# VectorE makes all low parts of the weights in two passes

## The reference, cut to what matters

```python
def conv_ffn(x, w_in, conv_w, conv_b, w_out):
    h = causal_depthwise_conv(x @ w_in, conv_w, conv_b)
    val, gate = jnp.split(h, 2, axis=-1)
    return (jax.nn.silu(gate) * val) @ w_out
...
        h = rms_norm(x, norm_mix_g[layer])
        if m == 0:
            y = pool_mixer(h, pool_w[j], pool_b[j], pool_scale[j])
        x = x + y.astype(x.dtype)
        f = conv_ffn(rms_norm(x, norm_ffn_g[layer]), ffn_w_in[layer], ffn_conv_w[layer], ffn_conv_b[layer], ffn_w_out[layer])
        x = x + f.astype(x.dtype)
```

## Time and profile before

| | |
|---|---|
| median of three runs | 2387.79 us |
| profiled execution | 2391.25 us, span 2389.5 us |
| TensorE busy | 2289.1 us, 96% |
| VectorE busy | 1600.5 us, 67% |
| ScalarE busy | 1313.9 us, 55% |
| GpSimd busy | 752.2 us, 31% |
| low parts on GpSimd (L2820) | 496.1 us in the page's largest group, 638 instructions |

### The profile page before, as it was taken

One profiled execution on the slowest core, in us unless ns is written; L12 is line 12 of the kernel. 1 busy time (PEld: TensorE's weight loads), 2 busy tenths in 40 slices (PEclk: granted clock), 3 DMA queues, 4 the chain that ended last, 5 costly groups with the idle time before them and its releaser, 6 DMA issues.

```text
span 2389.5 us, 35445 instructions
## 1 busy us (share of the span) xinstructions
PE 2289.1 (96%) x11782; PEld 1941.9 (81%) x11782; DVE 1600.5 (67%) x3239; ACT 1313.9 (55%) x3030; POOL 752.2 (31%) x909
## 2 busy tenths in 40 slices
PE   7999999999999999999999999898998999999999
PEld 6888777878887878888888888787777888887887
DVE  7443667667886423346655566568779788889787
ACT  6444556666775434446565566555555555455532
POOL 5555222311235652221222221558774300000000
PEclk9999999999999999999999999999999999999999
DMA  7322101111234342222332323532353633345734
GB/s 224 112 75 65 38 23 36 27 34 43 64 106 124 92 138 67 91 69 84 93 88 75 93 86 95 180 93 80 89 163 93 203 106 111 104 143 181 227 110 140
DMA packets 333316, 242.73 MB, mean 102 GB/s; under 512 B 66384, under 2 KB 286800, under 8 KB 332624
## 3 DMA queue, kind: packets, MB, share of 16 engines
q1 hardware_dynamic: 333136, 240.47, 33.1%
HBM read 196.64 MB, written 43.78 MB: 101 GB/s over the span
## 4 chain that ended last, share of the span: by engine, by line
PE 75%; DVE 11%; ACT 4%; issue 4%; POOL 3%; DMA 1%; SPq 1%; DVEq 0%; POOLq 0%; ACTq 0%
PE PS L1920 14%; PE PS L1922 13%; PE PS L1921 13%; PE PS L2159 6%; PE PS L2160 6%; PE PS L2161 6%; PE PS L2066 5%; PE PS L2033 5%; PE PS L2020 3%; PE PS L2021 2%; ACT PY L2170 2%; POOL WS L2820 1%; PE PS L2075 1%; POOL HT L2879 1%; DVE EO L2643 1%
## 5 line engine op out<-in xcount | busy, mean ns | idle before, releaser
L2820 POOL TENSOR_TENSOR WS<-WR,WS 128x256 fp32r<-128x256 f32 x638 | 496.1, 796 | 991.6 <-ACT WS L2170 990.4
L1920 PE MATMUL PS<-HT,WS 128*128 128x512 f32 x1488 | 603.7, 406 | 26.2 <-DVE X L2462 5.4
L1922 PE MATMUL PS<-HT,WS 128*128 128x512 f32 x1488 | 585.4, 393 | 0.0
L1921 PE MATMUL PS<-HT,WS 128*128 128x512 f32 x1488 | 583.5, 392 | 0.0
L1920 PEld LDWEIGHTS PS<-HT,WS 128*128 128x128 f32 x1488 | 282.0, 189 | 85.8 <-issue 20.3
L1922 PEld LDWEIGHTS PS<-HT,WS 128*128 128x128 f32 x1488 | 281.5, 189 | 61.7
L1921 PEld LDWEIGHTS PS<-HT,WS 128*128 128x128 f32 x1488 | 282.7, 190 | 52.1
L2170 ACT ACTIVATE PT<-PS 128x512 fp32r<-128x512 f32 x352 | 185.9, 528 | 225.8 <-PE PS L2033 225.5
L2170 ACT ACTIVATE WS<-WR 128x256 fp32r<-128x256 f32 x662 | 247.0, 410 | 96.4 <-PE PS L1922 56.4
L2418 DVE TENSOR_TENSOR PT<-PS,PT 128x512 fp32r<-128x512 f32 x352 | 211.0, 609 | 69.2 <-ACT PT L2170 66.9
L2066 PE MATMUL PS<-PT,QKV 128*128 128x256 f32 (+1 forms) x1248 | 209.8, 290 | 3.2 <-DVE YB L2597 2.3
(11 more groups left out here) (288 smaller groups left out, 4658.1 us busy)
## 6 DMA issues: line engine op xcount, KB each, us to landing
WR<-in_w_in_odd SPq DMA_DIRECT2D x106, 256.0 KB, 2.9
EO<-in_grid SPq DMA_DIRECT2D x48, 384.0 KB, 3.1
WR<-in_ffn_in SPq DMA_DIRECT2D x64, 256.0 KB, 3.0
WR<-in_w_in_even SPq DMA_DIRECT2D x100, 128.0 KB, 2.5
WR<-in_w_out_odd SPq DMA_DIRECT2D x48, 256.0 KB, 2.9
yd<-PY SPq DMA_DIRECT2D x44, 256.0 KB, 3.3
EO<-in_ffn_in SPq DMA_DIRECT2D x35, 256.0 KB, 3.1
WR<-in_w_in_even SPq DMA_DIRECT2D x34, 256.0 KB, 2.9
```

What stands on the lines that cost most here:

```text
L1920: e.matmul(out, wh, rh, start=start, stop=False)
L1921: e.matmul(out, wh, rl, start=False, stop=False)
L1922: return e.matmul(out, wl, rh, start=False, stop=stop)
L2820: e.tensor_tensor(ws(i, 1, n), RAW[raw_slot(u)][:, o:o + n], f32(ws(i, 0, n)), ALU.subtract).then_inc(s_wlop.sem, 1)
```

## The change

The flag that says from which piece on VectorE makes low parts is now set before the first pass instead of before the second, and the condition "every fourth piece" is gone. VectorE makes the low parts of all 136 pieces of the two passes and of the pooling products that lie in the first. The place in the list of steps where a low part stands is the same as before.

```diff
-        at = {..., "second": None}
+        at = {..., "passes": None}
...
-                    on = s_wlov if at["second"] and no >= at["second"] and no % 4 == 3 else s_wlop
+                    on = s_wlov if at["passes"] and no >= at["passes"] else s_wlop
...
                 if 2 <= oc < 6:
                     pool_task(0, oc - 2)
+            at["passes"] = len(subs)
             for i in range(2 * PLAIN):
                 half_task(i // 2, HID * (i % 2), 0)
                 if i in (4, 6, 8, 9):
                     pool_task(1, (4, 6, 8, 9).index(i))
-            at["second"] = len(subs)
             for i in range(2 * PLAIN):
                 half_task(i // 2, HID * (i % 2), 1)
```

More of the change, by code:

```diff
@@ L366, in build @@
         units, subs, half_lo, used = [], [], [], {}
-        at = {"load": 0, "split": 0, "both": 0, "bank": 0, "ys": 0, "slot": 0, "task": 0, "gen": None, "piece": 0, "rope": False, "f1": False, "one": False, "deep": None, "second": None}
+        at = {"load": 0, "split": 0, "both": 0, "bank": 0, "ys": 0, "slot": 0, "task": 0, "gen": None, "piece": 0, "rope": False, "f1": False, "one": False, "deep": None, "passes": None}
         raw_at = []
```

## The result

The kernel after took 2397.68 us, the median of six runs (2395.59 to 2402.21), beside 2388.78 us for the kernel before on the same chips: a ratio of 1.0037 (95% interval 1.0026 to 1.0047), 8.9 us slower. A second measurement gave 1.0031 (1.0020 to 1.0041). The forecast was 2392.7 us, 4.9 us slower, in a range of 2383 to 2402. The way was right, the size was a little over half.

The account below looks back on a forecast made before the run. TensorE was taken as the pace from 1675 to 1900 us, VectorE next, its late queue causing waits. Stretch terms 0 + 0 + 2.0 + 2.9 + 0 gave +4.9 us, so 2392.7 us; range 2383 to 2402.

Parts of the forecast that it names:

- Cost of a low part on VectorE: In VectorE's queue the next instruction starts 0.33 us after a low part; taken as 0.34 us each.
- Relief, 0.14 us each: Time VectorE's stretched two-input SBUF instructions regain per low part leaving GpSimd, 0.14 us; net cost then 0.20 us each.
- 1711 to 1764: 0: Pooled blocks of the second half: added VectorE work and earlier L2879 cancel, about 0 us; bounds -4.9 to +5.8.
- The signs in the prediction: What the trace after should show, such as TensorE's wait for L2718 about 10 us and for L2879 near 4.
- 1782 to 1812.5: +2.0: Up to L2718: 14 low parts at 0.20 us, less 0.8 of wait; TensorE waits 2.0 us longer.
- 1812.5 to 1857: +2.9: After 1822.5: 17 low parts at 0.20 us, less 0.5; TensorE held at the same low part as before.
- The faster rival: Passes: relief equals cost, 0.34 us each, and both L2879 waits go, 4.9 us; 2383 us; chance 0.20.
- The clearly slower rival: In VectorE's order each low part waits for ScalarE's high part, +7 us more in full stretches; 2400 us; chance 0.16.
- The advice to give VectorE the elementwise work: Skill's rule that GpSimd is about twice slower (trace 0.738 against 0.413 us); by it alone the edit would gain.

Follow-up runs that it names:

- only second pass: Kernel before with only the second pass's other low parts moved to VectorE, GpSimd keeping the first pass's: 1.0014, 2394.21 beside 2390.56 us.
- thinned kernel after: Kernel after with VectorE's sums for the quarters stepped at every second weight piece instead of each: 1.0023 against the kernel before, 5.5 us slower.

## Why the prediction was right, point by point

- **Cost of a low part on VectorE.** Right. From one start to the next it is 0.33 us in the kernel after too:

```profile
1813.21 0.42 DVE L2449 TENSOR_TENSOR WS<-WR,WS 128x256 fp32r<-128x256 f32 x1
1813.54 0.75 DVE L2716 SCALAR_TENSOR_TENSOR SG<-PS,COL,SG 128x511 f32<-128x511 f32 x1
1814.33 0.75 DVE L2718 SCALAR_TENSOR_TENSOR SG<-PS,COL,SG 128x510 f32<-128x510 f32 x1
```

- **Relief, 0.14 us each.** Wrong in every stretch, and both ways. For the same VectorE instructions in both traces, the time that each got shorter adds up to 8.7 us from 1711 to 1764 for 31 low parts, 0.28 each; to 1.4 us from 1782 to 1812.5 for 16, 0.09 each; and to 4.9 us from 1812.5 to 1857 for 18, 0.27 each. The second profile gives the same three sums. In the first stretch the running sum (L2689) was stretched as well, from 1.28 to 1.80 us; with the carried value it never ran undisturbed before, so its least told me nothing. Between 1782 and 1812 GpSimd's norm work stayed: L2650 kept its 1.67 us, and a low part that met that work took 1.31.

- **1711 to 1764: 0.** Right in the sum: from 1691.9 to 1770.0 the first profile gains 0.8, the second 0.2. The waits for L2879 went as the argument had it; GpSimd began block 7's low part at 1759.88 instead of 1762.39. (The signs in the prediction had that wait stay near 4 us; it went.) But TensorE then waited for L2800, which stands in VectorE's order behind three low parts. One wait took the other's place, 3.3 us for 3.8. VectorE's queue itself fell back by only 0.5 us against the kernel before from 1711 to 1763.8; relief, and 4.2 us of idle time that went, took up the rest.

```profile
1759.88 2.32 POOL L2879 TENSOR_TENSOR HT<-EO,HT 128x512 fp32r<-128x512 f32 x1 [4.25 <-ACT HT L2170]
```

```profile
1762.43 0.41 DVE L2449 TENSOR_TENSOR WS<-WR,WS 128x256 fp32r<-128x256 f32 x1
1762.77 1.40 DVE L2800 SCALAR_TENSOR_TENSOR X<-PS,COL,X 128x512 f32<-128x512 f32 x2
```

- **1782 to 1812.5: +2.0.** It was 3.2, because of the missing relief. The same wait as forecast, 11.4 us where I had said 10. The sum closes with what was measured: 14 x 0.33 = 4.6, 0.9 for the low part that met GpSimd's norm work, less 1.4 of relief and 0.8 of the wait that VectorE had, 3.3 us. In this stretch the mechanism is right.

- **1812.5 to 1857: +2.9.** It was some 2 and 1.4 in the two profiles, and it was not VectorE's net work. Between its same instructions from 1822.5 to 1854 VectorE took 31.6 us before and 31.3 after, with 12 low parts more: here relief equals cost. TensorE was not held at the low part that held it before (matmul at 1858.18, 0.7 us) but 18 matmuls earlier, for 1.9 us, at a piece whose low part GpSimd had made in time. In VectorE's order it stands behind the second tap and one of the sums for the quarters. The same wait at the same matmul is in "only second pass". So the forecast's number was near here by luck.

- **What failed: the stretches began too late.** I took the sum from 1711 on and put nothing before it. The first low parts of the change stand at 1676 to 1690, before VectorE's low parts of a norm (L2650) for which TensorE waits. Eight of them stand there, and L2650 followed (before, then after):

```profile
1691.93 0.50 PE L1920 MATMUL PS<-HT,WS 128*128 128x512 f32 x1 [0.61 <-DVE HT L2650]
```

```profile
1692.31 0.50 PE L1920 MATMUL PS<-HT,WS 128*128 128x512 f32 x1 [1.88 <-DVE HT L2650]
```

That was 1.3 to 1.6 us, and in one of two profiles a clock at its lower level behind it. It is a missing term, but not the whole difference. In the first profile the errors are +1.6 here, -0.8 up to 1770, +1.2, -0.9 and -0.5 after 1858, which brings +4.9 to +5.5. They cancel in good part, so the nearness of the sum to the traces is partly luck. The traces account for 5.5 and 5.8 of the measured +6.7 and +8.9; the rest of the timed difference stays open.

- **The faster rival** (the shared ports cost more than VectorE's time). Relief would have to be 0.34 each everywhere; it was 0.28 at best over a whole stretch, and reached 0.33 only from 1822.5 to 1854, where a new wait took its place. L2705 took 1.16 us with GpSimd's low parts beside it and 0.685 without. The rule of the Trainium skill (SBUF — State Buffer, Who interferes with whom), an exclusive lock on a shared port pair, holds here. But the prediction had VectorE always as the one that is held up, and it is so only where GpSimd's instruction began first (last section). The rule doesn't say how often two instructions meet, and that set the price.

- **The clearly slower rival** (each low part waits for its high part). VectorE waited 1.2 us at 96 low parts from 1697 to 1862. Out, except at the pass's end in the thinned kernel after. Its price in the prediction left out a row of the same view: before, VectorE also waited 5.3 us at one low part in PT, so 10.2 us at nine and not 4.9 at eight. The longest wait of this kind was known, and it is the one that cost time there.

- **The advice to give VectorE the elementwise work** (the Trainium skill, GPSIMD Engine Reference, Engine selection) led the wrong way here: the instruction got faster, 0.42 for 0.74 us, and the kernel slower.

## What to carry to other kernels

An instruction that costs half as much on another engine is still a loss if that engine's queue is the late one: count the full stretches of the engine that takes the work, net of what the other one's going gives back, and start counting where its first instruction stands, not where the busy part begins. Then look at each moved instruction's place in the new queue: TensorE lost 1.9 us at a piece that had been ready, though VectorE's queue took no longer there. Before a difference of 1 to 2 us between two profiles is explained, take a second profile of the same kernel. When a long wait names a buffer, free the buffer and look whether short waits take its place; if they do, spread the late engine's work first, and only then does the free buffer pay.

## What the runs showed of the hardware

Which engine begins first decides who pays. In the kernel before, from 1600 to 1900, I took the instructions of seven lines of VectorE with two SBUF inputs (L2449, L2607, L2650, L2705, L2724, L2737, L2742). Each that began while one of GpSimd's was running took longer by the time that GpSimd's still had to run, less 0.13 us (0.126 to 0.139 in all 61 cases with over 0.2 us to run). At 1857.09 a low part took 0.95 instead of 0.41 us; GpSimd's, begun earlier, had 0.67 us to run. One of GpSimd's subtractions of 128 x 256 so costs up to 0.55 us. In the 18 cases where GpSimd's alone began later, VectorE's took at most 9 ns longer; GpSimd's subtraction took 0.93 to 1.00 us instead of 0.74 where both ran for 0.33 to 0.41 us. Five of the six running sums with a carried value were stretched by 0.37 to 0.50 us, and nothing that read PSUM was (L2716 0.741 before, 0.744 after). After a wait of TensorE of 3.8 us the granted clock was at its lower level for some 6 us, during which matmuls are 0.43 us apart; removing the wait removed that too. A wait therefore can cost more than its length: the one of 3.8 us cost 6.4, and 4.8 in the profiles where 5 matmuls and not 13 were at the lower level.
